# Delta rule's doublings on the 32 occupied columns of each head's 64: products, masks, copies and sums

## What is computed

```python
def step(state, inp):
    r_t, w_t, k_t, v_t, aa_t, bb_t = inp
    sa = jnp.einsum('bhij,bhj->bhi', state, aa_t)
    state = (state * w_t[:, :, None, :] + sa[..., None] * bb_t[:, :, None, :]
             + v_t[..., None] * k_t[:, :, None, :])
    y = jnp.einsum('bhij,bhj->bhi', state, r_t)
    return state, y
```

## Time and profile before

| | |
|---|---|
| median of 3 runs | 2138.1 us (2137.19 to 2140.96) |
| the profiled execution | 2141.78 us, its span 2140.0 us |
| busy in the span | TensorE 2106.1 us (98%), VectorE 903.0, ScalarE 892.3, GpSimd 894.2 |
| rwkv_chunks | from about 280 to 422 us of the span |
| granted TensorE clock | 0.995 of full speed over the span |

### The profile page before, as it was taken

One profiled execution on the slowest core, in us unless ns is written; L12 is line 12 of the kernel. 1 busy time (PEld: TensorE's weight loads), 2 busy tenths in 40 slices (PEclk: granted clock), 3 DMA queues, 4 the chain that ended last, 5 costly groups with the idle time before them and its releaser, 6 DMA issues.

```text
span 2140.0 us, 30849 instructions
## 1 busy us (share of the span) xinstructions
PE 2106.1 (98%) x12648; PEld 1710.3 (80%) x12648; DVE 903.0 (42%) x1523; ACT 892.3 (42%) x1681; POOL 894.2 (42%) x692
## 2 busy tenths in 40 slices
PE   8999999999999999999999999999999999999998
PEld 6767788888888888877777888888887788888886
DVE  4222666444530121153336744442237864444222
ACT  4344643434542243243336444443245535444322
POOL 4523320025344444454232444444454345444543
PEclk9999999999999999999999999999999999999999
DMA  7222210024232233312111133322222122333321
GB/s 270 92 79 84 70 41 18 12 81 142 77 101 99 90 98 99 99 60 89 52 58 60 50 99 99 99 98 91 97 69 98 60 79 79 99 99 99 99 97 61
DMA packets 53589, 184.10 MB, mean 86 GB/s; under 512 B 5816, under 2 KB 5824, under 8 KB 53320
## 3 DMA queue, kind: packets, MB, share of 16 engines
q1 hardware_dynamic: 53448, 182.13, 25.7%
HBM read 176.84 MB, written 8.15 MB: 86 GB/s over the span
## 4 chain that ended last, share of the span: by engine, by line
PE 93%; DVE 3%; DMA 1%; ACT 1%; issue 1%; POOL 1%; SPq 0%; POOLq 0%; ACTq 0%; DVEq 0%
PE ps L351 22%; PE ps L352 22%; PE ps L353 22%; PE ps L2757 2%; PE ps L2759 2%; PE ps L2758 2%; PE ps L377 2%; PE ps L371 1%; PE ps L372 1%; PE ps L1120 1%; DMA raw_units<-stream 1%; PE ps L1629 1%; PE ps L485 1%; PE ps L1122 1%; PE ps L1121 1%
## 5 line engine op out<-in xcount | busy, mean ns | idle before, releaser
L200 POOL TENSOR_TENSOR split_units<-raw_units,split_units 128x512 fp32r<-128x512 f32 x628 | 818.9, 1329 | 1108.1 <-ACT split_units L177 1091.3
L177 ACT ACTIVATE split_units<-raw_units 128x512 fp32r<-128x512 f32 x624 | 356.8, 621 | 366.7 <-PE ps L353 334.5
L351 PE MATMUL ps<-x_split,split_units 128*128 128x512 f32 x1208 | 475.2, 393 | 1.7 <-DVE work L2420 0.8
L353 PE MATMUL ps<-x_split,split_units 128*128 128x512 f32 x1208 | 470.8, 390 | 0.0
L352 PE MATMUL ps<-x_split,split_units 128*128 128x512 f32 x1208 | 470.8, 390 | 0.0
L351 PEld LDWEIGHTS ps<-x_split,split_units 128*128 128x128 f32 x1208 | 227.3, 188 | 54.3 <-issue 4.0
L352 PEld LDWEIGHTS ps<-x_split,split_units 128*128 128x128 f32 x1208 | 227.4, 188 | 47.9 <-issue 1.4
L353 PEld LDWEIGHTS ps<-x_split,split_units 128*128 128x128 f32 x1208 | 227.2, 188 | 47.6
L351 PE MATMUL ps<-hidden_split,split_units 128*128 128x512 f32 x608 | 237.3, 390 | 0.0
L353 PE MATMUL ps<-hidden_split,split_units 128*128 128x512 f32 x608 | 236.6, 389 | 0.0
L352 PE MATMUL ps<-hidden_split,split_units 128*128 128x512 f32 x608 | 236.5, 389 | 0.0
(11 more groups left out here) (522 smaller groups left out, 3295.8 us busy)
## 6 DMA issues: line engine op xcount, KB each, us to landing
raw_units<-stream SPq DMA_DIRECT2D x314, 512.0 KB, 3.7
work<-gate_rows SPq DMA_DIRECT2D x12, 256.0 KB, 2.8
bias_rows<-bias_line SPq DMA_DIRECT2D x1, 2816.0 KB
gate_rows<-work SPq DMA_DIRECT2D x10, 256.0 KB, 2.1
x<-x_t SPq DMA_DIRECT2D x4, 512.0 KB, 7.0
work<-bias_rows SPq DMA_DIRECT2D x1, 2048.0 KB
out_t<-x SPq DMA_DIRECT2D x8, 256.0 KB
vec<-vectors SPq DMA_DIRECT2D x1, 1159.5 KB, 8.4
```

Source lines behind the costliest of these rows:

```text
L177: scalar.activation(self.split[:, u % SPLIT, 0, part], self.raw[:, u % RING, part], ACT.Copy).then_inc(self.high_done, 1)
L200: gpsimd.tensor_tensor(self.split[:, u % SPLIT, 1, part], self.raw[:, u % RING, part], self.split[:, u % SPLIT, 0, part].bitcast(F32), ALU ...
L351: TE.matmul(out, high, rhs(0, k), start=(k == 0), stop=False)
L353: ins = TE.matmul(out, low, rhs(0, k), start=False, stop=last and shift is None)
```

## The change

A level's product x can be other than zero only in the columns in front: of each block of 2s columns the first s, 32 of a head's 64. The change makes every step of levels 1 to 5 take those alone:

- `x_block` streams the 32 front columns of T and writes them packed, 32 to a head, so the bank holds 128 columns and not 256;
- `mask_x` reads those 128 and writes them to their places in XX (a pattern with runs of s elements); the constant "levels" holds 32 columns a level;
- `t_block` streams the 32 front columns of XX and accumulates into the 32 front columns of the bank (runs of s in PSUM); `level_t` on ScalarE copies those 128 columns;
- `u_block` streams the other 32 columns of U, those behind, into a packed bank; `add_u` becomes a SCALAR_TENSOR_TENSOR on 128 columns, u = bank * level_rows + u, since rows that the mask used to keep at zero are now masked in the sum;
- the columns of XX that are no longer written must be zero: at the stage's start VectorE gets a memset of 128x256 for each group, and in every chunk ScalarE writes zeros (128x256) ahead of each `unity`.

The number of matmuls and their order, the 64 stationary columns of each, and the waits stay as they are. The diff, its core:

```diff
+            def blocks_of(ap, l, behind):
+                return ap.rearrange("p (a b s) -> p a b s", b=2, s=1 << l)[:, :, behind, :]
+            def packed(ap, l):
+                return ap.rearrange("p (a s) -> p a s", s=1 << l)
+            def four_by(ap, l, n):
+                return ap.rearrange("p (h a s) -> p h a s", h=4, s=n << l)[:, :, :, 0:1 << l]
...
-                def x_block(g, i, r):
-                    return TE.matmul(ps[home(g, r), 4 * g + 1, i * HD:(i + 1) * HD], n4(g, i, 0, r, r.start, HD),
-                                     tt(g, i, r), start=True, stop=True)
+                def x_block(l, g, i, r):
+                    return TE.matmul(packed(ps[home(g, r), 4 * g + 1, i * HHD:(i + 1) * HHD], l),
+                                     n4(g, i, 0, r, r.start, HD), blocks_of(tt(g, i, r), l, 0), start=True, stop=True)
...
-                    return TE.matmul(ps[r, 4 * g + 2, i * HD:(i + 1) * HD], uu(g, i, o), xx(g, i, o), start=False,
-                                     stop=(l == LAST - 1), skip_group_check=True)
+                    return TE.matmul(blocks_of(ps[r, 4 * g + 2, i * HD:(i + 1) * HD], l, 0), uu(g, i, o),
+                                     blocks_of(xx(g, i, o), l, 0), start=False, stop=(l == LAST - 1),
+                                     skip_group_check=True)
...
+                def u_block(l, g, i, o):
+                    return TE.matmul(packed(ps[o, 4 * g, i * HHD:(i + 1) * HHD], l), xx(g, i, o),
+                                     blocks_of(uu(g, i, o), l, 1), start=True, stop=True)
...
-                        V.tensor_tensor(four(w[:, XX[g], 0:256]), four(bank(4 * g + 1, 0, 256)),
-                                        wide(c("levels", (l - 1) * HD, HD)), ALU.mult).then_inc(dve_s[g].sem, 1)
+                        V.tensor_tensor(four_by(w[:, XX[g], 0:256], l, 2), four_by(bank(4 * g + 1, 0, P), l, 1),
+                                        keep, ALU.mult).then_inc(dve_s[g].sem, 1)
...
-                        V.tensor_tensor(w[:, UT[g], UNITY], w[:, UT[g], UNITY], bank(4 * g, 0, 256),
-                                        ALU.add).then_inc(dve_s[g].sem, 1)
+                        u = blocks_of(w[:, UT[g], UNITY], l, 1)
+                        V.scalar_tensor_tensor(u, packed(bank(4 * g, 0, P), l), c("level_rows", l - 1, 1), u,
+                                               ALU.mult, ALU.add).then_inc(dve_s[g].sem, 1)
...
                 for g in range(2):
+                    V.memset(w[:, XX[g], 0:256], 0.0)
                     dve_chain.link(dve, V.tensor_copy(four(w[:, UT[g], UNITY]), wide(c("ident64"))))
...
-                    S.activation(w[:, UT[g], 0:256], bank(4 * g + 2, 0, 256), ACT.Copy).then_inc(act_s[g].sem, 1)
+                    S.activation(blocks_of(w[:, UT[g], 0:256], l, 0), blocks_of(bank(4 * g + 2, 0, 256), l, 0),
+                                 ACT.Copy).then_inc(act_s[g].sem, 1)
...
                 def unity(g, ch):
+                    zero(w[:, XX[g], 0:256])
                     S.activation(four(w[:, UT[g], UNITY]), wide(c("ident64")), ACT.Copy).then_inc(act_s[g].sem, 1)
```

More of the change, by code:

```diff
@@ L71 @@
            ("pool_w", 512)]
-CONSTANTS = [("ident", 128), ("same_head", 128), ("levels", HD * (LEVELS - 2)),
-             ("level0_t", HD), ("ident64", HD), ("mask4", 512), ("diag_qk", 128), ("diag_st", 128), ("inv_count", 64), ("eps", 3)]
+CONSTANTS = [("ident", 128), ("same_head", 128), ("levels", HD // 2 * (LEVELS - 2)),
+             ("level_rows", LEVELS - 2), ("level0_t", HD), ("ident64", HD), ("mask4", 512), ("diag_qk", 128), ("diag_st", 128), ("inv_count", 64), ("eps", 3)]
 def merge_order():
@@ L1540, in uf @@
                 return w[r, UF[g], :].rearrange("p (a t) -> p a t", a=4)[:, :, a:a + HD]
+            HHD = HD // 2
             UPPER, LOWER = half(0), half(1)
@@ L1621, in moved_block @@
                               start=True, stop=True)
-                def x_block(g, i, r):
-                    return TE.matmul(ps[home(g, r), 4 * g + 1, i * HD:(i + 1) * HD], n4(g, i, 0, r, r.start, HD),
-                                     tt(g, i, r), start=True, stop=True)
+                def x_block(l, g, i, r):
+                    return TE.matmul(packed(ps[home(g, r), 4 * g + 1, i * HHD:(i + 1) * HHD], l),
+                                     n4(g, i, 0, r, r.start, HD), blocks_of(tt(g, i, r), l, 0), start=True, stop=True)
                 def t_block(l, g, i, r):
                     o = home(g, r)
-                    return TE.matmul(ps[r, 4 * g + 2, i * HD:(i + 1) * HD], uu(g, i, o), xx(g, i, o), start=False,
-                                     stop=(l == LAST - 1), skip_group_check=True)
-                def u_block(g, i, o):
-                    return TE.matmul(ps[o, 4 * g, i * HD:(i + 1) * HD], xx(g, i, o), uu(g, i, o), start=True,
-                                     stop=True)
+                    return TE.matmul(blocks_of(ps[r, 4 * g + 2, i * HD:(i + 1) * HD], l, 0), uu(g, i, o),
[4 more added lines that the diff above has]
+                                     blocks_of(uu(g, i, o), l, 1), start=True, stop=True)
                 def turn(g, ch):
@@ L1661, in level_x @@
                         for r in (UPPER, LOWER):
-                            ins = x_block(g, i, r)
+                            ins = x_block(l, g, i, r)
                     ins.then_inc(pe_s[g].sem, 1)
@@ L1681, in level_t_x @@
                         for r in (UPPER, LOWER):
-                            ins_x = x_block(h, i, r)
+                            ins_x = x_block(l_x, h, i, r)
                     ins_t.then_inc(pe_s[g].sem, 1)
@@ L1689, in level_u @@
                         for o in (UPPER, LOWER):
-                            ins = u_block(g, i, o)
+                            ins = u_block(l, g, i, o)
                     ins.then_inc(pe_s[g].sem, 1)
@@ L1849, in step @@
                         wait_pe(dve, g, ch, pe_level(l, "x"))
-                        V.tensor_tensor(four(w[:, XX[g], 0:256]), four(bank(4 * g + 1, 0, 256)),
-                                        wide(c("levels", (l - 1) * HD, HD)), ALU.mult).then_inc(dve_s[g].sem, 1)
+                        keep = packed(c("levels", (l - 1) * HHD, HHD), l).unsqueeze(1).to_broadcast(
+                            [P, 4, HHD >> l, 1 << l])
+                        V.tensor_tensor(four_by(w[:, XX[g], 0:256], l, 2), four_by(bank(4 * g + 1, 0, P), l, 1),
+                                        keep, ALU.mult).then_inc(dve_s[g].sem, 1)
                     return step
@@ L3790, in constant_array @@
         levels.append((row // (2 * s) == colm // (2 * s)) & (row % (2 * s) >= s) & (colm % (2 * s) < s))
-    put("levels", np.concatenate([np.tile(m[:HD, :HD], (2, 1)) for m in levels[1:LEVELS - 1]], axis=1))
+    in_front = [np.flatnonzero(np.arange(HD) % (2 << l) < 1 << l) for l in range(1, LEVELS - 1)]
+    put("levels", np.concatenate([np.tile(levels[l][:HD, in_front[l - 1]], (2, 1)) for l in range(1, LEVELS - 1)],
+                                 axis=1))
+    put("level_rows", np.stack([i % (2 << l) < 1 << l for l in range(1, LEVELS - 1)], axis=1))
     put("level0_t", np.tile(levels[0][:HD, :HD].T, (2, 1)))
```

## The result

The changed kernel takes 2147.5 us (median of 20 runs, 2137.4 to 2156.7), the kernel before 2139.0 (20 runs, 2135.3 to 2141.7): ratio 1.0039, 95% interval 1.0026 to 1.0052. The profiled execution took 2140.7 us, the second shortest of the 20.

| mean clock | changed kernel, us |
|---|---|
| 0.997 | 2137.4 |
| 0.996 to 0.994 | 2140.7, 2141.0, 2141.5, 2142.6 |
| 0.993 to 0.991 | 2143.0 to 2149.5 (8 runs) |
| 0.990 to 0.987 | 2151.6 to 2156.7 (7 runs) |

What follows compares the result with a forecast made beforehand. The prediction took a 1.27 us loop of dependent matmuls and VectorE's mask to bound the levels. Saving 5.8 us over 36 steps and losing 0.35 to memsets gave 2132.6 us against 2138.1, range 2129.5 to 2138.0.

Steps and rivals of the forecast that it cites:

- Does anything beside the ring take over?: Levels' steps: ScalarE, VectorE and TensorE's issue stay under the new 1.105 us step, so 36 x 0.162 = 5.8 us saved.
- The matmuls: Levels' t, x, u matmuls: weight loads set the pace, halved columns save only the last matmul's tail, 25 ns a step.
- the three things by which the prediction said it would be wrong: In the levels: a round's spacing moves, short runs cost VectorE, or ScalarE's copy of T releases the x matmuls.
- What bounds the kernel: Levels: a dependent loop of matmuls and mask, 1.27 us a step, sets the pace; 36 of 40 masks on the path.
- the ring: One level step: eight t and x matmul rounds, last matmul, handover, VectorE's mask, handover back; 1.27 us.
- I take 0 off the rounds: Levels' matmul rounds: every weight load stays, so halving the streamed columns leaves the round's 0.059 us unchanged.
- rival 1: Levels' matmul rounds shrink too because moving columns set them: steps of 0.90 us, 2123.6 us in all; chance 0.08.
- rival 3: Levels' matmuls with broken columns run slower, streaming overtaking the weight load: 2157 us at four times the price; chance 0.06.
- The mask, the copy, the sum: Levels, VectorE and ScalarE: mask 424 to 287 ns, saving 137; copy of T 384 to 274; sum 419 to 344.
- Rival 2: VectorE's mask: short runs eat the saving, mask stays near 424 ns, 2137.5 us; chance 0.16 with its middle cases.
- What is added: ScalarE's zeros in each chunk are free; VectorE's two memsets at the stage's start lose 0.35 us, once.
- Sum: Whole kernel: -5.8 + 0.35 = -5.5 us; profiled execution 2136.3 us, median 2132.6 us, 0.26% less.

Runs made afterwards that it cites:

- narrow_slow: The changed kernel with a longer ring: VectorE masks head 0 alone ahead of each mask, all matmuls narrow; 2156.6 us, ratio 1.0078.
- again: The changed kernel run once more without any edit, for its spread and a second trace; 2147.6 us, ratio 1.0047.
- more_instr: The kernel before with the u matmuls of heads 0 and 1 issued once more in each step, same result; 2148.1 us, ratio 1.0042.
- less_instr: whole_cols without the u products and sums of heads 2 and 3, so its result is not the reference's; 2131.9 us, ratio 0.9966.
- whole_cols: The changed kernel with all level matmuls streaming 64 columns again, masks, copies and sums still at 128; 2137.9 us, ratio 0.9997.
- x_cols: The changed kernel with only the x product streaming all 64 columns, mask still 128x128; 2139.0 us, ratio 1.0004.
- u_cols: The changed kernel with only the u product streaming all 64 columns, x and t narrow; 2139.0 us, ratio 1.0001.
- x_whole: The changed kernel with x product and 128x256 mask as in the kernel before, t and u narrow; 2140.1 us, ratio 1.0001.

## Why the prediction was wrong, step by step

Two steps failed. "Does anything beside the ring take over?" left out that TensorE's instructions must be brought in time (5.1 us of stalls in the sections, 0.9 behind one), and "The matmuls" put the streamed columns at nothing, with which the clock went (6.8 us on the median). None of the three things by which the prediction said it would be wrong came; of what it expected to see, the four sections' sum is off, 44.95 us against 40.5, and the first turn a little, 0.15 us later against 0.3 to 0.45.

- **What bounds the kernel.** Right as far as it went: the ring sets the step, 36 steps are on the path. Not seen: a bound close above it.
- **The matmuls.** "I take 0 off the rounds" held: at 32 columns a round still takes 0.058 us (337.40 to 337.81 is seven), so rival 1 and rival 3 are both out. At level 1, where the runs in PSUM are of 2 elements, it is the same (293.34 to 293.74 is seven). The Trainium skill, "TensorE: Matmul & The Clock Gate", section "Back-to-back issue gap", has in its table one gap for 1 to 64 columns; the prediction took the formula above it alone, and by the table it does not speak for rival 1. The rounds agree, 0.058 us at 32 columns and 0.059 at 64. The Trainium skill, "PSUM — Partial Sum Buffer", section "Specifications (TRN2)", would have slowed them; every undisturbed step of 1.107 us speaks against it here, where whole pairs are written. What failed is that a column that costs no time was taken to be worth nothing. In these kernels the clock goes with the streamed columns: with half of them in all three products it fell to 0.50 for up to 24 us at a time (narrow_slow), with one product whole the mean stayed at 0.995 to 0.997 in 33 executions. The prediction gave the clock no term; from the profiled execution (2140.7) to the median (2147.5) it is 6.8 us, the larger of the two errors. The Trainium skill, "TensorE: Matmul & The Clock Gate", warns of idle gaps between bursts of matmuls (section "Why this matters for your kernels"); here TensorE shows as busy 10.5 of 12.3 us before the fall in `again`, with no idle time longer than 0.91 us, and the clock fell all the same.
- **The mask, the copy, the sum.** Right: 292, 279, 349 ns. Rival 2 is out.
- **"Does anything beside the ring take over?"** This step failed. ScalarE, VectorE and TensorE's rounds were counted, and none took over; the bringing of TensorE's instructions was not. The 0.8 us of "single stalls" of before, four steps longer by 0.12 to 0.25 us, were seen and not asked after. The step itself is 1.107 us, against 1.105 computed. But 5.1 us of stalls came, 4.3 more than before, and left 1.4 us of the 5.8; the stall behind chunk 0's section took 0.9 of these. more_instr (7.5 us more of stalls at a step of 1.267), less_instr (0.8 us of stalls at 1.134) and the packets' times show the mechanism.
- **What is added.** The zeros on ScalarE are free: `output` starts at 315.61, the next transposes at 316.82. The memsets take 0.27 us each, as computed, and VectorE's first `unit_blocks` starts 0.46 later after the transposes' start, but the first turn only 0.15 (4.02 us after the transposes at 283.25; before 3.87 after those at 283.90): 0.2 better than the 0.35 forecast.
- **Sum.** In the profiled execution: 1.4 us gained in the sections, 0.9 lost behind chunk 0's, 0.15 lost at the start, so 0.4 us for the change where 5.5 were forecast. The span is 1.1 us shorter (2138.9 against 2140.0); the other 0.65 was there before the stage began (transposes at 283.25 against 283.90) and is luck. Against the 2136.3 forecast for this execution, 2140.7 is 4.4 more, the 5.1 us that the change fell short of its 5.5, less that 0.65. The clock adds up to 16 us to it, by the run. For the median the miss is 14.9 us (2147.5 against 2132.6): these 4.4, the 6.8 of the clock, and 3.7 by which the profiled execution of before lay above its median.

What stays open: what sets the pace of the instruction packets, and why TensorE goes on 1.2 to 1.6 us after the end of one; no experiment moved the fetching itself, only the number of instructions. What in the chip ties the clock to the streamed columns is not shown either, and not every execution or chunk of the narrow kernels falls: chunks 2 and 3 of narrow_slow's profile keep the full clock through their levels. No kernel between the changed one and those with one product whole was tried, nor t whole alone.

## What to carry to other kernels

When a loop is a ring of short dependent matmuls, count its instructions per microsecond as a resource beside the engines' time: here 96 matmul and weight-load records in 1.27 us, 76 per us, were about all that TensorE was given over four sections, and of the 4.8 to 5.8 us that a faster ring promised the sections gave 0.1 to 2.4 until the count fell. Where the idle time says "issue", lay it beside the times of the instruction packets. Columns that ride free behind a weight load need not be cut: look at the granted clock of every run, not only of the profiled one, before removing work that costs no time. A change whose profiled execution looks level can be slower in most of its runs.

## Not expected of the hardware

- The clock at 0.50 for 13.65 us twice in one execution (again), for 23.9 us twice in another (narrow_slow: 295.65 to 319.55 and 340.03 to 363.92 us), on a TensorE that shows as busy all through these stretches. The profile of the kernel before has low stretches too, outside the stage; one is behind it, 6.83 us from 434.60, with matmuls of 2 moving columns (L2071) from 432.43 on.
- At the lower clock a round of small matmuls takes about twice as long though only 32 columns are streamed: sixteen u records take 1.04 us there (narrow_slow) against 0.63, a round of some 0.11 us against 0.058.
- Over its four level sections TensorE got 75 to 78 matmul and weight-load records per us, whatever the ring asked for, unless it asked for less: before 75 (3463 / 46.38), whole_cols 75 (3456 / 46.31), x_cols 76 (3452 / 45.66), the changed kernel 77 (3451 / 44.95), u_cols 78 (3452 / 43.98), more_instr 75 (4039 / 53.90). Single sections lie further apart, the changed kernel's chunk 0 at 83 (867 / 10.45). The kernels with under 1 us of stalls ask for no more than that: before 96 / 1.267 = 76, x_whole 96 / 1.241 = 77, less_instr 80 / 1.134 = 71; the changed kernel asks for 87.
